# Layer norms of a four-layer decoder trunk: root and reciprocal on whole rows in place of five-column statistics

## Chip, cores and metric

The kernel runs as one launch on one core of a Trainium2 chip (trn2). The metric is the time of one execution on the device in microseconds; smaller is better. Engines are named as the profile names them: PE is TensorE's matmul stream and PEld its weight loads, DVE is VectorE, ACT is ScalarE, POOL is GpSimd, SP is SyncE, which issues the weight loads from memory.

## What is computed

The reference is one inference step of a trunk of four layers over 512 prompt tokens and 8 decode tokens, 520 columns in all, with a model width of 1024. Layers 0 and 3 mix tokens by multi-scale retention, layer 1 by causal pooling over windows, layer 2 by sparse attention that a small indexer selects. After each mixer and after each SwiGLU stands a residual with a layer norm, so there are eight norms. The part that matters here:

```python
def layer_norm(x, g, b):
    xf = x.astype(F32)
    mu = jnp.mean(xf, axis=-1, keepdims=True)
    var = jnp.mean(jnp.square(xf - mu), axis=-1, keepdims=True)
    return ((xf - mu) * lax.rsqrt(var + LN_EPS) * g.astype(F32) + b.astype(F32)).astype(x.dtype)

def deepnorm_residual(x, h, g, b):
    return layer_norm(DEEPNORM_ALPHA * x + h, g, b)
...
        xp = deepnorm_residual(xp, hp, ln_g[i, 0], ln_b[i, 0])
...
        xp = deepnorm_residual(xp, swiglu(xp, ffn_w_in[i], ffn_w_out[i]), ln_g[i, 1], ln_b[i, 1])
```

## The kernel before

The activations lie transposed: `x` holds 128 rows of partitions by 8 chunks of 520 columns, so a token is a column and its 1024 features are spread over 128 partitions and 8 chunks. A sum over features is therefore a matmul with the constant matrix `avg`, which gives every partition the mean over all of them.

All large products are made in a three-term split. A weight block of 128 rows by 1024 columns (a *unit*) is loaded by SP into one of four slots of `w_raw`. ACT rounds it to its high part (`split_hi`, L514 to L518), DVE subtracts to get the low part (`split_lo`, L520 to L526), and PE then makes 48 matmuls of 260 columns from it (`multiply`, L536 to L549). `split_next` (L528) splits the unit that stands two places ahead, as soon as the products of the present one are done. The high and low parts have two halves of a ring as their home, so a unit normally has to wait until the unit two places before it is multiplied; `home` (L508) gives only unit 2 of the stage `first` a third place.

Every engine has its own program, a list of stages, and they meet at semaphores. A norm, `norm0a` to `norm3b` (a after the mixer, b after the SwiGLU), goes as follows before the change:

- The last products of the stage before are added to `x` chunk by chunk on DVE (`z_add`, L1732, L1763, L2235 or L2237). After each, DVE adds the chunk to `sum_s` (L1462) and its square, which ACT makes at L1076, to `sum_q` (L1465).
- PE (`norm`, L2958) fills its waiting time with idle products (`hold`, L2955; not in `norm0b` and `norm3b`), spreads the mean over all partitions with `avg` (L2966) and then makes mean and mean square once more in turned form: for five groups of 128 columns it gives one column each (L2972), so that the 520 numbers stand as 128 rows by 5.
- DVE (`norm`, L2253) subtracts the mean from the first four chunks (`less_mean`, L2259), works out the variance on 128x5 (L2267 to L2274); ACT takes the root (L1383), DVE the reciprocal (L2276).
- PE spreads the 128x5 back to all partitions and 520 columns with 12 small products (L2983).
- DVE multiplies each chunk by that (L2307) and, between two of these, subtracts the mean from one of the remaining three chunks and makes the low part of a normed chunk (`x_lo`, L1436). ACT applies gain and bias and makes the high part (L1389, L881).
- PE starts the next stage with `multiply_first` (L563 to L592), which follows the chunks of `x_h` and `x_l` as they come (L578).

One unit of the next stage's weights is split on DVE behind the reciprocal (L524).

The stage `idx` (layer 2, `index`, L2654 on PE) projects four units for the indexer; the first three are turned by a rotation product (L2652, `d_rotate` on DVE, L1821 to L1824). The stage `ret` (layers 0 and 3) starts on ACT with the scaling of the whole `x` by the residual factor (L896).

## Time and profile before

| quantity | value |
|---|---|
| time, median of 3 runs | 3108.71 us (3106.39 to 3112.1) |
| the profiled execution's own time | 3100.85 us |
| its span, first to last instruction | 3099.2 us |
| PE busy | 2963.1 us, 96% |
| PEld busy | 2789.9 us, 90% |
| DVE busy | 2022.0 us, 65% |
| ACT busy | 1250.1 us, 40% |
| POOL busy | 209.1 us, 7% |
| mean granted TensorE clock | 0.976 |

Busy shares are shares of the span. The granted clock is a share of 2.4 GHz: 1.00 is 2.4 GHz, 0.50 is 1.2 GHz, and a value between them is a mean over a stretch in which both occurred. Matmuls overlap, so where the text needs what one matmul costs, it takes the distance between starts and not the duration.

### The profile page before, as it was taken

What the parts mean: (1) busy time and instruction counts of PE and PEld (TensorE: products, weight loads), DVE (VectorE), ACT (ScalarE), POOL (GpSimd) and SP (SyncE); (2) the same over time, 40 slices, a digit from 0 to 9 for tenths busy, and PEclk for the clock granted to TensorE, in tenths of its full rate; (3) what the DMA queues carried; (4) which work ended last, traced back from release to release, by engine and by line L of the source; (5) the groups of instructions that cost most, each with busy time, mean ns of one, the idle gap of its engine ahead of it and who ended that gap; (6) DMA issues with size and microseconds to landing.
All of it is one profiled execution on the core that took longest, in us unless ns stands there. A gap on an engine that the chain in (4) does not pass through costs nothing.

```text
span 3099.2 us, 54122 instructions
## 1 busy us (share of the span) xinstructions
PE 2963.1 (96%) x22655; PEld 2789.9 (90%) x22655; DVE 2022.0 (65%) x3062; ACT 1250.1 (40%) x1881; POOL 209.1 (7%) x342
## 2 busy tenths in 40 slices
PE   7999999999996999998898899999999999999998
PEld 7898987899995999987797799999989888899998
DVE  4555556858567856767886486857555554685766
ACT  3332342535344634433343153534533333263543
POOL 0102111000000000011011100000020111000000
PEclk9999999999997999999998999999999999999998
DMA  6344444233331333332122423333344534323332
GB/s 155 130 126 154 132 131 131 79 103 103 96 92 39 89 96 109 91 99 58 50 74 79 133 69 103 103 96 96 99 144 125 162 126 149 109 82 97 109 94 64
DMA packets 492948, 323.77 MB, mean 104 GB/s; under 512 B 29723, under 2 KB 469275, under 8 KB 492698
## 3 DMA queue, kind: packets, MB, share of 16 engines
q1 hardware_dynamic: 465906, 230.14, 26.6%
q0 software_dynamic: 26800, 90.18, 8.4%
q8 instruction: 180, 2.95, 0.4%
q14 instruction: 62, 0.51, 0.1%
HBM read 275.90 MB, written 44.82 MB: 103 GB/s over the span
## 4 chain that ended last, share of the span: by engine, by line
PE 89%; DVE 7%; ACT 2%; issue 2%; DMA 0%; POOL 0%; DVEq 0%; SPq 0%; ACTq 0%; POOLq 0%
PE ps L547 46%; PE ps L2887 8%; PE ps L2888 8%; PE ps L2889 8%; PE ps L2345 2%; PE ps L597 2%; PE ps L578 2%; PE ps L598 2%; PE ps L599 2%; PE ps L2478 2%; PE ps L2468 1%; ACT w_h L518 1%; DVE wf L2259 1%; DVE wf L2307 1%; PE ps L2972 1%
## 5 line engine op out<-in xcount | busy, mean ns | idle before, releaser
L547 PE MATMUL ps<-rr,w_h 128*128 128x260 f32 x3776 | 608.7, 283 | 1.0 <-DVE rr L2073 1.0
L524 DVE TENSOR_TENSOR w_l<-w_raw,w_h 128x1024 fp32r<-128x1024 f32 (+2 forms) x312 | 336.7, 1079 | 402.2 <-ACT w_h L518 401.1
L547 PEld LDWEIGHTS ps<-rr,w_h 128*128 128x128 f32 x3776 | 518.0, 189 | 7.7 <-issue 5.6
L518 ACT ACTIVATE w_h<-w_raw 128x1024 fp32r<-128x1024 f32 (+2 forms) x312 | 293.3, 940 | 487.0 <-PE ps L547 458.6
L547 PE MATMUL ps<-x_h,w_h 128*128 128x260 f32 x2128 | 443.9, 290 | 7.6 <-DVE w_l L524 5.2
L547 PE MATMUL ps<-x_h,w_l 128*128 128x260 f32 x2128 | 430.9, 284 | 0.0
L547 PE MATMUL ps<-x_l,w_h 128*128 128x260 f32 x2128 | 430.6, 284 | 0.0
L547 PE MATMUL ps<-rr,w_l 128*128 128x260 f32 x1888 | 380.9, 283 | 0.0
L2887 PE MATMUL ps<-x_h,w_h 128*128 128x260 f32 x1280 | 362.0, 283 | 2.2 <-DVE w_l L2111 2.2
L2888 PE MATMUL ps<-x_l,w_h 128*128 128x260 f32 x1280 | 361.5, 282 | 0.0
L2889 PE MATMUL ps<-x_h,w_l 128*128 128x260 f32 x1280 | 361.0, 282 | 0.0
L547 PEld LDWEIGHTS ps<-x_h,w_h 128*128 128x128 f32 x2128 | 332.0, 191 | 32.3 <-issue 23.7
L547 PEld LDWEIGHTS ps<-x_l,w_h 128*128 128x128 f32 x2128 | 331.3, 190 | 0.0
L547 PEld LDWEIGHTS ps<-x_h,w_l 128*128 128x128 f32 x2128 | 330.6, 190 | 0.0
L547 PEld LDWEIGHTS ps<-rr,w_l 128*128 128x128 f32 x1888 | 291.7, 189 | 0.0
L2887 PE MATMUL ps<-rr,w_h 128*128 128x260 f32 x960 | 271.2, 282 | 1.2 <-ACT wf L1301 0.9
L2888 PE MATMUL ps<-rr,w_h 128*128 128x260 f32 x960 | 270.7, 282 | 0.0
L2889 PE MATMUL ps<-rr,w_l 128*128 128x260 f32 x960 | 270.3, 282 | 0.0
L2887 PEld LDWEIGHTS ps<-x_h,w_h 128*128 128x128 f32 x1280 | 240.8, 188 | 3.1 <-DVE w_l L2111 3.1
L2889 PEld LDWEIGHTS ps<-x_h,w_l 128*128 128x128 f32 x1280 | 241.5, 189 | 0.0
L2888 PEld LDWEIGHTS ps<-x_l,w_h 128*128 128x128 f32 x1280 | 240.8, 188 | 0.0
L1258 ACT ACTIVATE w_h<-w_raw 128x1024 fp32r<-128x1024 f32 x160 | 169.7, 1061 | 134.5 <-PE ps L2889 100.6
(349 smaller groups left out, 5017.0 us busy)
## 6 DMA issues: line engine op xcount, KB each, us to landing
w_raw<-in_ffn_w_in SPq DMA_DIRECT2D x176, 512.0 KB, 4.1
w_raw<-in_ret_w_in SPq DMA_DIRECT2D x96, 512.0 KB, 3.8
out<-wf POOLq DMA_DIRECT2D x72, 512.0 KB, 3.5
wf<-in_state_ret POOLq DMA_DIRECT2D x64, 512.0 KB, 5.7
w_raw<-in_ffn_w_out SPq DMA_DIRECT2D x64, 512.0 KB, 4.3
w_raw<-in_ret_w_out SPq DMA_DIRECT2D x64, 256.0 KB, 2.9
w_raw<-in_dsa_w_in SPq DMA_DIRECT2D x27, 512.0 KB, 3.8
w_raw<-in_ffn_w_out SPq DMA_DIRECT2D x32, 384.0 KB, 3.6
```

The source lines that it names most:

```text
L518: C.activation(whole(stage, k, home(w_h, stage, k, n)[:, 0:m]), landed(stage, k, n, m), ACT.Copy).then_inc(S["w_hi"], 1)
L524: V.tensor_tensor(whole(stage, k, home(w_l, stage, k, n)[:, 0:m]), landed(stage, k, n, m), whole(stage, k, home(w_h, stage, k, n)[:, 0:m]. ...
L547: mm = M.matmul(ps[:, 2 * (n % 2) + b, 0:HALF], lhs[:, c, :], rhs[:, c, cols], start=(c == 0 and term == 0), stop=(c == cs - 1 and term == 2))
L578: mm = M.matmul(ps[:, 2 * n + b, 0:HALF], lhs, rhs[:, c, cols], start=(c == 0 and term == 0), stop=(c == DC - 1 and term == 2))
L597: M.matmul(out, lhs_h, rhs_h, start=start, stop=False)
L598: M.matmul(out, lhs_h, rhs_l, start=False, stop=False)
L599: return M.matmul(out, lhs_l, rhs_h, start=False, stop=stop)
L1258: C.activation(w_h[:, a * Q:e * Q], src[:, 0:(e - a) * Q], ACT.Copy).then_inc(S[f"g{g}_hi"], 1)
L2345: return M.transpose(out, src, ident[0:n, 0:n])
L2887: M.matmul(out, wh, hi[:, c], start=fresh and c == 0, stop=False, skip_group_check=True)
L2888: M.matmul(out, wh, lo[:, c], start=False, stop=False, skip_group_check=True)
L2889: mm = M.matmul(out, wl, hi[:, c], start=False, stop=c == 3, skip_group_check=True)
```

## The change

Six things change together.

1. PE no longer makes the turned statistics and no longer spreads the 128x5 back. It spreads the mean and the mean square over all partitions and 520 columns with `avg`, into four banks.
2. The last chunk is not added to `sum_s` and `sum_q` by DVE. PE adds it, as a second accumulating product of `avg` with `x[:, 7]` and with its square.
3. ACT squares the mean (520 columns), DVE forms the variance, clamps it, ACT takes the root and DVE the reciprocal, all on 128x520.
4. `EARLY` goes from 4 to 2: two chunks have their mean subtracted before the reciprocal, and six between the products behind it. The splits of the next stage's first two units move: one to the head of the norm, one behind the first multiplication by the reciprocal.
5. Unit 2 of `idx` and `ret` gets the third home, as `first` has it, and is split at the head of its stage. The order of rotations, copies and splits in `idx` changes.
6. The scaling of `x` in `ret` moves on ACT from the head of the stage to the place behind the fifth unit's evacuation.

The diff, cut to its core:

```diff
-EARLY = 4
+EARLY = 2
...
+        def third(stage, i, k):
+            return kind_of(stage) in ("first", "idx", "ret") and (i, k) == (0, 2)
...
-            if then and kind_of(then[0]) != "fast":
+            if then and kind_of(then[0]) != "fast" and not third(*then):
...
             def ret(stage):
                 act.wait_ge(*at0("x_hi", 0))
-                C.activation(x[:], x[:], ACT.Copy, scale=ALPHA).then_inc(S["xs"], 1)
+                split_hi(act, stage, 0, 2)
...
                     step(4, lambda: raw_v(0))
+                    if i == 0:
+                        C.activation(x[:], x[:], ACT.Copy, scale=ALPHA).then_inc(S["xs"], 1)
...
             def norm(stage, which):
                 at = marks.here(stage)
-                act.wait_ge(*at("ln_v", 4))
-                C.activation(lve, lve, ACT.Sqrt).then_inc(S["ln_sd"], 1)
+                act.wait_ge(*at("stat", 1))
+                C.activation(halves(mean_q), ps[:, 4:6, 0:HALF], ACT.Square).then_inc(S["ln_m"], 1)
+                act.wait_ge(*at("ln_v", 2))
+                C.activation(sum_q, sum_q, ACT.Sqrt).then_inc(S["ln_sd"], 1)
...
+                if m == DC - 1:
+                    return
                 dve.wait_ge(*at("sum_s", m))
...
             def index(stage):
                 at = marks.here(stage)
                 dve.wait_ge(*at("tab_in", 80))
-                for k in range(4):
-                    split_next(split_lo, dve, stage, 0, k)
-                    if k < 3:
-                        d_rotate(at, k, itab, k % 2, k % 2)
...
+                split_lo(dve, stage, 0, 2)
+                for k in range(3):
+                    d_rotate(at, k, itab, k % 2, k % 2, 4 + 2 * (k % 2))
+                    if k == 0:
+                        split_next(split_lo, dve, stage, 0, 1)
...
+                    if k < 2:
+                        split_next(split_lo, dve, stage, 0, k + 2)
...
             def norm(stage):
...
-                dve.wait_ge(*at("stat", 1))
-                dve.wait_ge(*at("sum_q", 0))
+                last = last_unit(stage)
+                if last:
+                    split_next(split_lo, dve, *last[0:2], last[2] - 1)
+                dve.wait_ge(*at("stat", 2))
+                dve.wait_ge(*at("ln_m", 1))
+                V.scalar_tensor_tensor(halves(sum_q), ps[:, 6:8, 0:HALF], EPS, halves(mean_q), ALU.add, ALU.subtract
+                                       ).then_inc(S["ln_v"], 1)
+                dve.wait_ge(*at("ln_v", 1))
+                V.tensor_scalar(sum_q, sum_q, EPS, None, ALU.max).then_inc(S["ln_v"], 1)
                 for c in range(EARLY):
                     less_mean(c)
-                dve.wait_ge(*at("stat", 2))
-                V.tensor_copy(lve, mean).then_inc(S["ln_v"], 1)
...
                 dve.wait_ge(*at("ln_sd", 1))
-                V.reciprocal(lrs, lve).then_inc(S["ln_rs"], 1)
-                if last_unit(stage):
-                    split_next(split_lo, dve, *last_unit(stage))
+                V.reciprocal(sum_q, sum_q).then_inc(S["ln_rs"], 1)
...
-                less_mean(EARLY)
-                dve.wait_ge(*at("ln_b", 1))
+                dve.wait_ge(*at("ln_rs", 1))
...
-                    V.tensor_tensor(halves(ln_e[:, c]), halves(ln_e[:, c]), ps[:, 6:8, 0:HALF], ALU.mult
+                    V.tensor_tensor(halves(ln_e[:, c]), halves(ln_e[:, c]), halves(sum_q), ALU.mult
                                     ).then_inc(S["ln_e"], 1)
-                    if c + EARLY + 1 < DC:
-                        less_mean(c + EARLY + 1)
+                    if c + EARLY < DC:
+                        less_mean(c + EARLY)
+                    if c == 0 and last:
+                        split_next(split_lo, dve, *last)
...
             def index(stage):
...
+                for k in range(2):
+                    pe.wait_ge(*at("d_raw", k + 1))
+                    rotate(at, k, roti, k % 2, 4 + 2 * k)
+                multiply(pe, stage, 0, 2, x_h, x_l, DC)
+                multiply(pe, stage, 0, 3, x_h, x_l, DC, range(2))
+                pe.wait_ge(*at("d_raw", 3))
+                pe.wait_ge(*at("d_rope", 3))
+                rotate(at, 2, roti, 0)
+                multiply(pe, stage, 0, 3, x_h, x_l, DC, range(2, DC))
...
             def norm(stage, before):
-                pe.wait_ge(*at("sum_s", 0))
-                for b, cols in enumerate(prompt_halves()):
-                    mm = M.matmul(ps[:, 4 + b, 0:HALF], avg[:], sum_s[:, cols], start=True, stop=True)
-                mm.then_inc(S["stat"], 1)
...
-                if held:
-                    hold(10)
...
+                for bank, total, added, part, ready in ((4, sum_s, "sum_s", x[:, DC - 1], "z_add"),
+                                                        (6, sum_q, "sum_q", sq[:, (DC - 1) % 2], "sq")):
+                    pe.wait_ge(*at(added, 0))
+                    for b, cols in enumerate(prompt_halves()):
+                        M.matmul(ps[:, bank + b, 0:HALF], avg[:], total[:, cols], start=True, stop=False)
+                    pe.wait_ge(*at(ready, 0))
+                    for b, cols in enumerate(prompt_halves()):
+                        mm = M.matmul(ps[:, bank + b, 0:HALF], avg[:], part[:, cols], start=False, stop=True)
                     mm.then_inc(S["stat"], 1)
```

What moves in the instruction lists is shown at three places. The first is DVE in `norm1b`, from the statistics to the first low part; `x` is the residual stream, `ps` the matmul banks, `w_l` the weights' low parts, and `wf` and `tiny` are work buffers. Before:

```order
L2259 TENSOR_TENSOR wf<-x,ps 128x520 [waits sum_q,stat]
L2259 TENSOR_TENSOR wf<-x,ps 128x520 x3
L2267 COPY tiny<-ps 128x5 [waits stat]
L2269 TENSOR_TENSOR tiny<-tiny 128x5 [waits ln_v]
L2272 TENSOR_TENSOR tiny<-ps,tiny 128x5 [waits ln_v,stat]
L2274 TENSOR_SCALAR tiny<-tiny 128x5 [waits ln_v]
L2276 RECIPROCAL tiny<-tiny 128x5 [waits ln_sd]
L524 TENSOR_TENSOR w_l<-w_raw,w_h 128x1024 [waits w_hi]
L2259 TENSOR_TENSOR wf<-x,ps 128x520
L2307 TENSOR_TENSOR wf<-wf,ps 128x520 [waits ln_d,ln_b]
L2259 TENSOR_TENSOR wf<-x,ps 128x520
```

And with the change:

```order
L526 TENSOR_TENSOR w_l<-w_raw,w_h 128x1024 [waits w_hi,z_add]
L2280 SCALAR_TENSOR_TENSOR wf<-ps,wf 128x520 [waits ln_m,stat]
L2283 TENSOR_SCALAR wf<-wf 128x520 [waits ln_v]
L2272 TENSOR_TENSOR wf<-x,ps 128x520 x2
L2287 RECIPROCAL wf<-wf 128x520 [waits ln_sd]
L2315 TENSOR_TENSOR wf<-wf 128x520 [waits ln_d,ln_rs]
L2272 TENSOR_TENSOR wf<-x,ps 128x520
L526 TENSOR_TENSOR w_l<-w_raw,w_h 128x1024 [waits w_hi]
L2315 TENSOR_TENSOR wf<-wf 128x520 [waits ln_d]
L2272 TENSOR_TENSOR wf<-x,ps 128x520
L1445 TENSOR_TENSOR x_l<-x,x_h 128x520 [waits x_n,x_hi]
```

Five instructions on 128x5 and the wait for PE's spreading (`ln_b`) have gone; the reciprocal is 520 wide, and one split has moved in front of the statistics and one behind the first multiplication.

The second place is PE in the same norm, from its idle products (L2955, now L2965) on. Before, up to the first of the twelve products that spread the 128x5 (thirteen more idle products follow them):

```order
L2955 MATMUL ps<-ident_r 128x256 x10
L2966 MATMUL ps<-wf,avg 128x260 [waits sum_s]
L2966 MATMUL ps<-wf,avg 128x260
L2972 MATMUL ps<-avg,wf 128x1 [waits sum_s]
L2972 MATMUL ps<-avg,wf 128x1 x4
L2972 MATMUL ps<-avg,wf 128x1 [waits sum_q]
L2972 MATMUL ps<-avg,wf 128x1 x4
L2955 MATMUL ps<-ident_r 128x256 x10
L2983 MATMUL ps<-ident,tiny 128x128 [waits ln_rs]
```

And with the change, up to the thirteen idle products:

```order
L2965 MATMUL ps<-ident_r 128x256 x10
L2978 MATMUL ps<-wf,avg 128x260 [waits sum_s]
L2978 MATMUL ps<-wf,avg 128x260
L2981 MATMUL ps<-x,avg 128x260 [waits z_add]
L2981 MATMUL ps<-x,avg 128x260
L2978 MATMUL ps<-wf,avg 128x260 [waits sum_q]
L2978 MATMUL ps<-wf,avg 128x260
L2981 MATMUL ps<-wf,avg 128x260 [waits sq]
L2981 MATMUL ps<-wf,avg 128x260
L2965 MATMUL ps<-ident_r 128x256 x13
```

Eight wide products stand in place of two wide and sixteen narrow ones, the ten idle products in the middle have gone, and the thirteen at the end now follow the statistics and not the spreading.

The third place is DVE at the head of `idx`, in the change; `wf` holds the rotated projections, and the three splits L526 without a wait for `tab_in` are those of unit 3 and of units 0 and 1 of the following stage `q`. The second rotation is the second row of L1833:

```order
L526 TENSOR_TENSOR w_l<-w_raw,w_h 128x1024 [waits w_hi,tab_in]
L1833 TENSOR_TENSOR wf<-ps,wf 128x520 [waits d_rope,rot]
L1834 TENSOR_TENSOR wf<-wf 128x520
L1836 TENSOR_TENSOR wf<-wf 128x520 [waits d_rope]
L526 TENSOR_TENSOR w_l<-w_raw,w_h 128x1024 [waits w_hi]
L1848 COPY wf<-wf 128x8 [waits d_rope]
L1851 TENSOR_TENSOR rr<-wf,rr 128x520 [waits d_hi]
L526 TENSOR_TENSOR w_l<-w_raw,w_h 128x1024 [waits w_hi]
L1833 TENSOR_TENSOR wf<-ps,wf 128x520 [waits d_rope,rot]
```

Before, the split of `q`'s unit 0 stood behind the second rotation and ahead of the third; now it stands ahead of the second, and that of unit 1 ahead of the third.

## Rows read from the trace of the kernel before

**Rows 1.** The profile page: the chain that ended last, by engine.
```profile
PE 89%; DVE 7%; ACT 2%; issue 2%; DMA 0%; POOL 0%; DVEq 0%; SPq 0%; ACTq 0%; POOLq 0%
```

**Rows 2.** Timeline of norm1b: start us, us, engine, line, operation, [idle before <-releaser].
```profile
1355.83 1.48 PE L2955 MATMUL ps<-ident_r 128*128 128x256 f32 x11
1356.03 0.70 DVE L2235 TENSOR_TENSOR x<-ps,x 128x520 f32<-128x520 f32 x1 [0.74 <-PE ps L547]
...
1357.52 1.14 PE L2966 MATMUL ps<-wf,avg 128*128 128x260 f32 x4 [0.21 <-DVE wf L1462]
1358.50 2.51 PE L2972 MATMUL ps<-avg,wf 128*128 128x1 f32 x20
...
1362.23 0.19 DVE L2276 RECIPROCAL tiny<-tiny 128x5 f32<-128x5 f32 x1 [0.27 <-ACT tiny L1383]
1362.33 1.18 DVE L524 TENSOR_TENSOR w_l<-w_raw,w_h 128x1024 fp32r<-128x1024 f32 x1
...
1364.91 0.69 DVE L2307 TENSOR_TENSOR wf<-wf,ps 128x520 f32<-128x520 f32 x1 [0.79 <-PE ps L2983]
1365.53 0.69 DVE L2259 TENSOR_TENSOR wf<-x,ps 128x520 f32<-128x520 f32 x1
```

**Rows 3.** Groups of instructions by line and form: count | busy us, mean ns of one.
```profile
L1482 DVE TENSOR_TENSOR wf<-wf,rtab 128x1040 f32<-128x1040 f32 x16 | 19.8, 1236 | 0.6
...
L2011 DVE RECIPROCAL tiny<-tiny 128x1 f32<-128x1 f32 x32 | 4.5, 142 | 5.8 <-ACT wf L1222 5.8
L2276 DVE RECIPROCAL tiny<-tiny 128x5 f32<-128x5 f32 x8 | 1.5, 190 | 2.2 <-ACT tiny L1383 1.9 <-ACT tiny L1366 0.3
...
L2274 DVE TENSOR_SCALAR tiny<-tiny 128x5 f32<-128x5 f32 x8 | 1.4, 170 | 0.3
...
L1532 DVE TENSOR_SCALAR wf<-wf,headc 128x520 f32<-128x520 f32 x32 | 15.4, 480 | 0.0
...
L1076 ACT ACTIVATE wf<-x 128x520 f32<-128x520 f32 x64 | 40.1, 627 | 42.0 <-DVE x L2235 17.8 <-DVE x L1763 11.8 <-DVE x L1732 7.4
```

**Rows 4.** Timeline of norm2a, norm0a, norm1a, norm0b: idle products or last addition, first multiplication.
```profile
1793.30 1.47 PE L2955 MATMUL ps<-ident_r 128*128 128x256 f32 x11
...
1801.51 0.69 DVE L2307 TENSOR_TENSOR wf<-wf,ps 128x520 f32<-128x520 f32 x1
...
549.48 1.52 PE L2955 MATMUL ps<-ident_r 128*128 128x256 f32 x11
...
562.14 0.70 DVE L2307 TENSOR_TENSOR wf<-wf,ps 128x520 f32<-128x520 f32 x1 [1.92 <-PE ps L2983]
...
986.71 2.71 PE L2955 MATMUL ps<-ident_r 128*128 128x256 f32 x11 [6.28 <-DVE x L1763]
...
998.14 0.69 DVE L2307 TENSOR_TENSOR wf<-wf,ps 128x520 f32<-128x520 f32 x1 [2.25 <-PE ps L2983]
...
920.04 0.70 DVE L2235 TENSOR_TENSOR x<-ps,x 128x520 f32<-128x520 f32 x1 [1.71 <-PE ps L547]
...
929.67 0.70 DVE L2307 TENSOR_TENSOR wf<-wf,ps 128x520 f32<-128x520 f32 x1 [1.65 <-PE ps L2983]
```

**Rows 5.** Timeline behind norm0a: PE's first product after `multiply_first`.
```profile
578.97 0.40 PE L547 MATMUL ps<-x_h,w_h 128*128 128x260 f32 x2
```

**Rows 6.** Stretches: us, busy per engine (x), PEclk, DMA share, GB/s; behind norm2a and norm2b.
```profile
1811.00:1815.00 4.00, 4.00 (x22) 4.00 (x22) 2.97 (x5) 3.94 (x6) 0.00 (x0) 0.58 0.00 0
2192.00:2195.00 3.00, 3.00 (x21) 3.00 (x21) 2.97 (x3) 0.00 (x0) 0.00 (x0) 0.71 0.96 345
```

**Rows 7.** Timeline: PE at unit 2 of `ret0` and `ret3`, then first rotation and transposes of `idx`.
```profile
39.41 0.48 PE L547 MATMUL ps<-x_h,w_h 128*128 128x260 f32 x2 [0.91 <-DVE w_l L524]
...
2191.74 0.48 PE L547 MATMUL ps<-x_h,w_h 128*128 128x260 f32 x2 [3.20 <-DVE w_l L524]
...
1382.64 1.04 PE L2652 MATMUL ps<-wf 128*128 128x260 f32 x4
...
1403.87 2.24 PE L2345 MATMUL ps<-ident,wf 128*128 128x128 f32 x10 [0.84 <-ACT wf L1118]
```

More of the change, by code:

```diff
@@ L373, in trunk @@
         ve, rs, mhalf = tiny[:, 40:45], tiny[:, 45:50], tiny[:, 50:51]
-        lve, lrs = tiny[:, 51:56], tiny[:, 56:61]
         hist, inv, tail = wf[:, 6240:7264], wf[:, 7264:7328], wf[:, 7328:8352]
@@ L506, in arrived, with home @@
             return S[f"w_in{slot_of(stage, i, k)}"], (marks.unit(stage, i, k) // 4 + 1) * 16
-        def home(w, stage, k, n):
-            if (kind_of(stage), k) == ("first", 2):
+        def third(stage, i, k):
+            return kind_of(stage) in ("first", "idx", "ret") and (i, k) == (0, 2)
+        def home(w, stage, i, k, n):
+            if third(stage, i, k):
                 return w[:, 5 * Q:7 * Q]
@@ L517, in split_hi @@
             act.wait_ge(*arrived(stage, i, k))
-            C.activation(whole(stage, k, home(w_h, stage, k, n)[:, 0:m]), landed(stage, k, n, m), ACT.Copy).then_inc(S["w_hi"], 1)
+            C.activation(whole(stage, k, home(w_h, stage, i, k, n)[:, 0:m]), landed(stage, k, n, m), ACT.Copy).then_inc(S["w_hi"], 1)
         def split_lo(dve, stage, i, k):
@@ L541, in multiply @@
                 pe.wait_ge(*unit_mark("w_lo", stage, i, k))
[L542 to L543 removed]
+            wh = home(w_h, stage, i, k, n).rearrange("p (c n) -> p c n", n=P)
+            wl = home(w_l, stage, i, k, n).rearrange("p (c n) -> p c n", n=P)
             for c in part:
@@ L1121, in index @@
                 at = marks.here(stage)
-                for k in range(4):
-                    if k >= 2:
-                        act.wait_ge(*at("d_rope", 3 * (k - 2) + 3))
-                    d_copy(at, k, stage, 0, k, k % 2)
-                    split_next(split_hi, act, stage, 0, k)
-                    if k < 3:
-                        act.wait_ge(*at("d_rope", 3 * k + 3))
-                        C.activation(qi_h[:, k, :] if k < 2 else ki_h, d_f[:, k % 2], ACT.Copy).then_inc(S["d_hi"], 1)
+                split_hi(act, stage, 0, 2)
+                d_copy(at, 0, stage, 0, 0, 0)
+                d_copy(at, 1, stage, 0, 1, 1)
+                split_next(split_hi, act, stage, 0, 1)
+                for k in range(3):
+                    act.wait_ge(*at("d_rope", 3 * k + 3))
+                    C.activation(qi_h[:, k, :] if k < 2 else ki_h, d_f[:, k % 2], ACT.Copy).then_inc(S["d_hi"], 1)
+                    if k < 2:
+                        d_copy(at, k + 2, stage, 0, k + 2, k)
+                        split_next(split_hi, act, stage, 0, k + 2)
                 act.wait_ge(*at("wi_tp", 1))
@@ L1345, in down @@
                 for k in range(8):
-                    if last and k == 7:
-                        square(at, at, k)
                     if k < 6 or not then:
@@ L1354, in down @@
                         lone_hi(stage, then)
-                    if last and k < 7:
+                    if last:
                         square(at, at, k)
@@ L1381, in norm @@
                 at = marks.here(stage)
-                act.wait_ge(*at("ln_v", 4))
-                C.activation(lve, lve, ACT.Sqrt).then_inc(S["ln_sd"], 1)
+                act.wait_ge(*at("stat", 1))
+                C.activation(halves(mean_q), ps[:, 4:6, 0:HALF], ACT.Square).then_inc(S["ln_m"], 1)
+                act.wait_ge(*at("ln_v", 2))
+                C.activation(sum_q, sum_q, ACT.Sqrt).then_inc(S["ln_sd"], 1)
                 for c in range(DC):
@@ L2254, in norm @@
                 at = marks.here(stage)
-                mean, square = (ps[:, 6 + n, STAT_AT:STAT_AT + QT + 1] for n in range(2))
                 def less_mean(c):
@@ L2659, in index @@
                 pe.wait_ge(*at("tab_in", 80))
-                for k in range(4):
-                    if k >= 2:
-                        pe.wait_ge(*at("d_raw", k - 1))
-                        multiply(pe, stage, 0, k, x_h, x_l, DC)
-                    if k < 3:
-                        pe.wait_ge(*at("d_raw", k + 1))
-                        if k:
-                            pe.wait_ge(*at("d_rope", 3 * k))
-                        rotate(at, k, roti, k % 2)
+                for k in range(2):
[7 more added lines that the diff above has]
+                multiply(pe, stage, 0, 3, x_h, x_l, DC, range(2, DC))
                 pe.wait_ge(*at("d_rope", 9))
```

71 lines of the change are left out of this document (25 added, 46 removed).

## Prediction, before the change was run

> **What bounds the kernel now.** I read the page first. The chain that ended last runs on PE for 89% of the span and on DVE for 7% [rows 1], so the kernel is one long stream of matmuls, and time is gained or lost only where PE has nothing useful to do. Such places are the norms and the heads of `ret` and `idx`, so I went through the timeline there.
>
> One norm shows the order of things [rows 2]. In `norm1b` the last chunk is added at 1356.03 and done 0.70 us later, at 1356.73. PE passes its idle products (from 1355.83, 1.48 us), spreads the mean at 1357.52, makes narrow statistics from 1358.50. The reciprocal on 128x5 starts at 1362.23. After PE has spread it back, DVE multiplies the first chunk at 1364.91, and PE's first useful product follows as soon as ACT has scaled it. The reader should see two distances: from the last addition to the first multiplication (8.2 us here), which the change rebuilds, and from the first multiplication to the end of `multiply_first`, which depends on how quickly DVE delivers chunks. The second is 578.97 - 562.14 = 16.83 us in `norm0a` [rows 4, 5].
>
> **New path up to the first multiplication.** PE: a product of 260 columns with `avg` runs as two passes. Four passes start at 1357.52 and the next row starts at 1358.50 [rows 2], so a pass takes 0.245 us. The change has 8 products, 16 passes, 3.92 us in a row behind the idle products, which take 1.38 us from start to the next free place; with 0.15 us until the result can be read, the mean square stands 5.45 us after the first idle product.
>
> Then comes a chain that is 520 wide throughout. DVE waits for the semaphore (0.05), forms the variance, priced as a 520-wide two-tensor operation (0.69 [rows 2]), waits again (0.04), clamps (0.48 at L1532 [rows 3], of which about 0.42 until the next can start) and subtracts two means (two times 0.61, the distance of 1364.91 and 1365.53 [rows 2]). That makes 2.42 us until the reciprocal can start. The root on ACT, priced as its 520-wide square, 0.63 [rows 3], runs beside the two subtractions and is ready first. ACT's square of the mean and the root's table load lie beside PE's last eight passes (8 x 0.245 = 2.0 us) and cost nothing; without that cover they would add up to those 2 us.
>
> **The reciprocal's price R decides.** No row shows a wide one. For ordinary operations width costs 1.05 ns per element: 0.69 us at 520 [rows 2], 1.236 at 1040 [rows 3]. At that rate and with nothing else, R is 0.69 us: the lower bound. The reciprocal goes from 142 ns at one element to 190 at five [rows 3], 12 ns per element, which gives 142 ns + 519 x 12 ns = 6.4 us: the upper bound. A nearer reading is what it occupies: the split behind the five-wide reciprocal starts 0.10 us later (1362.23, 1362.33 [rows 2]). A 520-wide operation occupies 0.61 us, 0.54 for its elements and about 0.065 fixed. So five elements take 0.035 to 0.04 us, 7 to 8 ns each, and 520 take about 4.2 us; with fixed part and tail **R = 4.4 us**. I take this, because it compares the same operation in the same place with the instruction behind it, and durations of tiny operations contain waits.
>
> A rule speaks to this. The Trainium skill, "VectorE: DVE Perf Modes", section "First, the fixed hardware budget", says that reciprocal is an iterative divide with a repeat count of 8. By it R would be about eight times the 0.54 us of a plain row, 4.3 us as an estimate, and by the plain row's own price 0.69: the sum below would differ by 29 us. The five-wide row sides with the rule, though it is only five wide.
>
> So the first multiplication stands 5.45 + 2.42 + 4.4 = 12.27 us after the first idle product. Norm by norm, against the old start [rows 2, 4]:
>
> - `norm1b`: 1355.83 + 12.27 = 1368.10 against 1364.91, +3.2. `norm2b` is of the same build, +3.2.
> - `norm2a`: 1793.30 + 12.27 = 1805.57 against 1801.51, +4.1.
> - `norm1a`: PE comes from 6.28 us without work and runs the idle products at half rate, 2.71 us instead of 1.48 [rows 4], that is at 1.2 GHz. I let half of the passes run so: 5.5 us instead of 3.92 and 2.75 for the idle products, 986.71 + 15.2 = 1001.9 against 998.14, +3.8.
> - `norm0a`: 549.48 + 12.27 = 561.75 against 562.14, -0.4; here DVE was late with its sums, and not adding the last chunk saves that. `norm3a` alike, -0.4.
> - `norm0b` has no idle products; four passes are done before the last addition ends at 920.74 and 12 follow: 920.74 + 0.05 + 2.95 + 0.15 + 2.42 + 4.4 = 930.7 against 929.67, +1.0. `norm3b` alike, +1.0.
>
> Sum: **+15.5 us**. This part moves by 8 us for each us of R.
>
> **Behind the first multiplication** DVE now subtracts six means instead of three and makes a split. Each chunk costs it three operations of 0.61, 1.83 us, against about 1.45 that ACT and PE need for one (12 products of 0.121). The second multiplication starts at 0.61 + 0.61 + 1.14 (the split) = 2.36, the seventh 5 x 1.83 later at 11.5, the eighth at 12.7. Its high part is ready at about 15.1 and PE then has 32 products left, 3.9 us: 19.1 us against 16.83, +2.25 in `norm0a`, `1b`, `2a`, `2b`, `3a`; without the split 18.0 in `norm1a`, +1.1. In `norm0b` three subtractions and a half-wide split go ahead of the last chunk, +2.1, and in `norm3b`, where PE's transposes hide part, +1.0. Sum: **+15.5 us**. It does not depend on R.
>
> **The heads of the stages.** In `ret3` PE waits 3.20 us for unit 2's low part and then runs at a granted clock of 0.71 (a mean of 1.2 and 2.4 GHz) [rows 6, 7] for two such stretches of 3 us: with the third home the wait goes, and 6 us x 0.29 = 1.7 with it, **-5 us**. In `ret0` the wait is 0.91 [rows 7], **-0.9**. The moved scaling is eight 520-wide rows of ACT, at most 8 x 0.63 = 5 us by [rows 3]. It now stands beside PE's unit 5, 48 products of 0.12, 5.75 us, and so costs nothing; if ACT came to it late, it could delay one evacuation by 1 to 2 us in each of the two stages. In `idx` PE gets from the first rotation at 1382.64 to the transposes at 1403.87 [rows 7], 21.2 us. Now: two rotations 2.0, unit 2 5.75, two chunks of unit 3, a rotation and the rest 6.75, done at 14.5. But DVE now has the split of `q`'s unit 0 ahead of the second rotation, and ACT cannot make its high part before unit 2 is multiplied: unit 2 ends at 7.75, ACT's copy and split take 1.65 (0.63 per 520 [rows 3]) and DVE's split 1.18 [rows 2], so DVE resumes at 10.6. The same follows behind unit 3 (14.5 + 2.85 = 17.4), and the third rotation, three operations of DVE, ends at 19.4. The stall is thus not removed but moved to the transposes: -1.9, of which PE, starting again at 1.2 GHz, takes about 0.9, **-1**.
>
> **Clock.** PE's thirteen idle products end about 7 us before its first product now. A stretch like that is followed by 1.2 GHz in `norm1a`. But in the next 10 us DVE sets the pace, and I charge +2 in all. In return `norm2a` already lost time so (0.58 over 4 us [rows 6]) and `norm1b` a little; that is now hidden behind DVE, -3.
>
> **Sum:** 15.5 + 15.5 - 5 - 0.9 - 1 + 2 - 3 = **+23 us**. On the profiled execution's own 3100.85 us that is 3123.9. This execution lies 7.9 us below the median of 3108.71 and below all three runs (3106.39 to 3112.1), so I put the sum on the median: **3131.7, say 3131 us**.
>
> **Rivals.**
> A. *The reciprocal streams like any wide row*, R = 0.69. Then 8 x 3.71 = 29.7 us go and the time is 3102. For it: 190 ns at five elements is only 20 ns more than the 170 of the scalar operation of the same width [rows 3], which a fixed surcharge would explain. Against it: the start-to-start distance. It decides from R below 0.75 us on; at 1.5 us the change is worth nothing. The Trainium skill, "Vector Engine (DVE) Microarchitecture Reference", section "3.2 Anatomy of a single slice", has the divide chain span all eight slices, which reads as one element per cycle and would give this case; no row here is wide enough to show it.
> B. *Something between*, R near 2 us: +3.8, 3112, no change that can be measured.
> C. *R as forecast or up to 6.4, and PE stays at 1.2 GHz through `multiply_first`.* Then PE needs 2.6 us per chunk, 25.6 us in place of 19.1, six norms by some 3 to 6.5: 3145 to 3170. For it: 7 us without work in six norms. Against it: 11 idle products brought `norm1a` back to 2.4 GHz.
>
> **How the numbers follow.** A measurement of this kernel tells changes of over 0.2%, 6.2 us, from none. Forecast 0.56 (3119 to 3140 by the bounds of the unmeasured parts), A 0.24, B 0.10, C 0.10. A lies at the edge of 0.2%: 0.19 of it faster, 0.05 the same. Faster 0.19, same 0.15 (B and that part of A), slower 0.66. The range of 8 in 10 runs from 3100, inside A, to 3145, where C begins; the forecast's own is 3119 to 3140.
>
> **What would show it.** Right: a reciprocal row of 128x520 at 4 to 5 us, eight times; first multiplications 10 to 12 us after the last addition in `norm1b` and `norm2a`; chunks in `multiply_first` 1.8 us apart with PE waiting on `x_h`; no wait before unit 2 in `ret3`; a wait of some 5 us before the transposes in `idx`. Wrong: a reciprocal row under 1 us, or a time under 3115.

## The result, and the profile of the changed kernel

The change makes the kernel **slower by about 11 us**: median 3118.62 us (3114.83 to 3122.28, 6 runs) beside 3106.67 us (3102.74 to 3112.1) of the kernel before on the same chip, a ratio of 1.0035, interval 1.0024 to 1.0046. The forecast was 3131 us (+23), range 3100 to 3145: direction and range hold, the size is off by half. The profiled execution took 3114.83 us, its span is 3112.3 us, 13.1 us more than before; the granted clock is 0.973 against 0.976. Both profiles are of the fastest execution that their kernel has here.

The page of the changed kernel: its span, the busy time of the engines, and the chain that ended last by engine:

```profile
span 3112.3 us, 53632 instructions
...
PE 2943.1 (95%) x22435; PEld 2764.5 (89%) x22435; DVE 2041.6 (66%) x3030; ACT 1260.5 (41%) x1889; POOL 209.1 (7%) x342
...
PE 87%; DVE 9%; ACT 2%; issue 2%; DMA 0%; POOL 0%; SPq 0%; DVEq 0%; ACTq 0%; POOLq 0%
```

PE works 20 us less than before (its old statistics were two wide and ten narrow products a norm, not sixteen as counted above, and six products spread the 128x5 in twelve passes) and holds a smaller share of the chain; DVE's share went from 7% [rows 1] to 9%. Its groups by form (busy us, mean ns of one) show with what:

```profile
L2287 DVE RECIPROCAL wf<-wf 128x520 f32<-128x520 f32 x8 | 27.2, 3395 | 0.0
L2272 DVE TENSOR_TENSOR wf<-x,ps 128x520 f32<-128x520 f32 x64 | 43.5, 689 | 0.0
```

The price that was in doubt is 3.40 us, eight times. Plain rows of the same width cost 0.69. The timeline of `norm1b` after, which answers to [rows 2]:

```profile
1360.46 1.48 PE L2965 MATMUL ps<-ident_r 128*128 128x256 f32 x11
1360.66 0.70 DVE L2250 TENSOR_TENSOR x<-ps,x 128x520 f32<-128x520 f32 x1 [1.97 <-PE ps L549]
1361.39 1.23 DVE L526 TENSOR_TENSOR w_l<-w_raw,w_h 128x1024 fp32r<-128x1024 f32 x1
...
1361.78 1.04 PE L2978 MATMUL ps<-wf,avg 128*128 128x260 f32 x4
1362.66 1.04 PE L2981 MATMUL ps<-x,avg 128*128 128x260 f32 x4
...
1365.49 0.70 DVE L2280 SCALAR_TENSOR_TENSOR wf<-ps,wf 128x520 f32<-128x520 f32 x1 [2.87 <-PE ps L2981]
...
1367.78 3.39 DVE L2287 RECIPROCAL wf<-wf 128x520 f32<-128x520 f32 x1
1371.21 0.70 DVE L2315 TENSOR_TENSOR wf<-wf 128x520 f32<-128x520 f32 x1
...
1372.43 1.22 DVE L526 TENSOR_TENSOR w_l<-w_raw,w_h 128x1024 fp32r<-128x1024 f32 x1
...
1373.57 0.69 DVE L2315 TENSOR_TENSOR wf<-wf 128x520 f32<-128x520 f32 x1
1373.75 0.77 PE L580 MATMUL ps<-x_h,w_h 128*128 128x260 f32 x2 [6.76 <-DVE w_l L526]
...
1375.40 0.69 DVE L2315 TENSOR_TENSOR wf<-wf 128x520 f32<-128x520 f32 x1
```

The reader should see three things. DVE waits 2.87 us (the bracket at 1365.49) while PE spreads the means, although it still has a split of weights to make, which it makes at 1372.43, on the path. The first multiplication comes 10.75 us after the first idle product (1371.21 - 1360.46). And the chunks behind it are 1.83 us apart (1373.57, 1375.40), three DVE operations each.

**Where the 13.1 us of the span arose.** For each norm I read, in both timelines, the start of the last product ahead of it, of DVE's first multiplication, and of the last product of `multiply_first` (in `norm0b` and `norm3b`, which have none, of the last multiplication). Distances in us, before and after:

| norm | to the first multiplication | change | forecast | from there to the end | change | forecast |
|---|---|---|---|---|---|---|
| 0a | 12.78, 10.89 | -1.89 | -0.4 | 16.71, 19.03 | +2.32 | +2.25 |
| 0b | 9.95, 9.73 | -0.22 | +1.0 | 6.07, 8.52 | +2.45 | +2.1 |
| 1a | 17.99, 18.73 | +0.74 | +3.8 | 16.69, 17.88 | +1.19 | +1.1 |
| 1b | 9.20, 10.87 | +1.67 | +3.2 | 17.61, 19.02 | +1.41 | +2.25 |
| 2a | 8.33, 10.86 | +2.53 | +4.1 | 19.24, 19.03 | -0.21 | +2.25 |
| 2b | 10.16, 10.87 | +0.71 | +3.2 | 16.71, 19.02 | +2.31 | +2.25 |
| 3a | 12.77, 10.94 | -1.83 | -0.4 | 16.72, 19.09 | +2.37 | +2.25 |
| 3b | 9.98, 9.79 | -0.19 | +1.0 | 7.27, 9.11 | +1.84 | +1.0 |
| sum | | **+1.5** | +15.5 | | **+13.7** | +15.5 |

The norms together cost 15.2 us more. The right half agrees with the forecast (its -3 for the clock in `1b` and `2a` shows there too); the left half is wrong by 14 us. The heads gained 0.9 us in `ret0`, 4.9 in `ret3` and 0.4 in `idx` (taken to the end of `proj`), 6.2 in all. The remaining +4 lies where nothing was changed: +3.3 later in `ret3`, +1.6 later in `ret0`, -0.6 in the pooling. Most of the 3.3 is in the last head of `ret3`. Stretches there, after and then before (columns as in [rows 6]):

```profile
2680.00:2686.00 6.00, 6.00 (x36) 5.69 (x35) 3.43 (x6) 2.14 (x4) 0.00 (x0) 0.72 0.15 44
2686.00:2692.00 6.00, 3.90 (x20) 3.81 (x20) 2.80 (x6) 0.86 (x2) 0.00 (x0) 0.72 0.17 44
```

```profile
2670.00:2676.00 6.00, 4.95 (x40) 4.61 (x40) 5.21 (x9) 2.98 (x5) 0.00 (x0) 1.00 0.15 45
2676.00:2682.00 6.00, 3.90 (x32) 3.70 (x32) 3.18 (x7) 1.19 (x3) 0.00 (x0) 1.00 0.16 46
```

The same instructions, with the same short waits of PE for DVE (1.05 and 2.10 us) among them, ran at a granted clock of 1.00 before and 0.72 after (a mean of 2.4 and 1.2 GHz). That took 3.0 us, and 0.3 a little earlier, back out of the 4.9. The tail of `ret0` lost its 1.6 the same way (0.72 from 522 to 528 us, where the kernel before had 1.00).

### The profile page after: what moved, and what is told of

The parts are those of the page before. It is cut to its first block, busy times and chain, and to the rows that moved or that the text cites. A ratio compares the mean times of both kernels' runs of the same rounds, so it can differ in the third digit from the quotient of the medians.

```text
span 3112.3 us, 53632 instructions
## 1 busy us (share of the span) xinstructions
PE 2943.1 (95%) x22435; PEld 2764.5 (89%) x22435; DVE 2041.6 (66%) x3030; ACT 1260.5 (41%) x1889; POOL 209.1 (7%) x342
## 4 chain that ended last, share of the span: by engine, by line
PE 87%; DVE 9%; ACT 2%; issue 2%; DMA 0%; POOL 0%; SPq 0%; DVEq 0%; ACTq 0%; POOLq 0%
PE ps L549 45%; PE ps L2897 8%; PE ps L2898 8%; PE ps L2899 8%; PE ps L2355 2%; PE ps L599 2%; PE ps L600 2%; PE ps L601 2%; PE ps L2488 2%; PE ps L580 2%; DVE wf L2272 1%; DVE wf L2315 1%; DVE wf L2287 1%; PE ps L2478 1%; ACT w_h L520 1%
## 5 line engine op out<-in xcount | busy, mean ns | idle before, releaser
L526 DVE TENSOR_TENSOR w_l<-w_raw,w_h 128x1024 fp32r<-128x1024 f32 (+2 forms) x312 | 337.1, 1081 | 390.1 <-ACT w_h L520 385.1
## 6 DMA issues: line engine op xcount, KB each, us to landing
w_raw<-in_ffn_w_in SPq DMA_DIRECT2D x176, 512.0 KB, 4.0
w_raw<-in_ret_w_in SPq DMA_DIRECT2D x96, 512.0 KB, 3.9
out<-wf POOLq DMA_DIRECT2D x72, 512.0 KB, 3.6
wf<-in_state_ret POOLq DMA_DIRECT2D x64, 512.0 KB, 5.4
w_raw<-in_ffn_w_out SPq DMA_DIRECT2D x64, 512.0 KB, 4.3
w_raw<-in_dsa_w_in SPq DMA_DIRECT2D x27, 512.0 KB, 3.9
```

What stands on the lines that cost most here:

```text
L526: V.tensor_tensor(whole(stage, k, home(w_l, stage, i, k, n)[:, 0:m]), landed(stage, k, n, m), whole(stage, k, home(w_h, stage, i, k, n)[:, ...
```

## Experiments

Twelve runs, eleven new kernels and the changed kernel once more, each beside the kernel before on the same chip. The median of the kernel before was 3106.52 us beside `recip_more`, `act_arsqrt`, `split_early` and `heads_only`, and 3107.03 beside the others. Distances per norm below run from the last product ahead of the norm to the last of `multiply_first`, as in the table (both halves added).

**More reciprocal** (`recip_more`). The first 260 columns are inverted twice more.

```diff
                 V.reciprocal(sum_q, sum_q).then_inc(S["ln_rs"], 1)
+                for n in (1, 2):
+                    dve.wait_ge(*at("ln_rs", n))
+                    V.reciprocal(sum_q[:, 0:HALF], sum_q[:, 0:HALF]).then_inc(S["ln_rs"], 1)
...
-                dve.wait_ge(*at("ln_rs", 1))
+                dve.wait_ge(*at("ln_rs", 3))
```

> The changed kernel with the reciprocal of the first 260 columns taken twice more behind the one of 520 (the value stays the same). Theory (DVE's chain sets the norms, and a reciprocal costs 6.5 ns per element): two rows of 128x260 of 1.7 to 1.75 us each, first multiplications 3.5 us later in all eight norms, chunks behind them still 1.83 us apart, so 8 x 3.5 = 28 us more: 3118.6 + 28 = 3146.6 us (3143 to 3150). Rival 1 (TensorE's clock sets them: the longer pause costs a longer stretch at 1.2 GHz): over 3155. Rival 2 (part of the reciprocal is hidden beside other work): under 3135.

Measured: 3141.51 us (3141.23 to 3141.84), ratio 1.0111, interval 1.0096 to 1.0126. Its groups by form:

```profile
L2290 DVE RECIPROCAL wf<-wf 128x260 f32<-128x260 f32 x16 | 28.4, 1778 | 0.5
L2287 DVE RECIPROCAL wf<-wf 128x520 f32<-128x520 f32 x8 | 27.1, 3394 | 0.0
```

Two widths give the line: (3394 - 1778) / 260 = 6.2 ns per element and 162 ns fixed. The norms grew by 3.6 us each (`norm1b` 33.52 against 29.89; `norm1a` 4.7), 30 us by the timelines in all eight. The total rose by 23 only: `ret3` took 3.3 us less here, its last head running at full rate, and this kernel's median lies 0.3 us above its profiled execution, that of the changed kernel 3.8. Rival 1 is out. The total is under the range of the theory and over that of rival 2; the norms themselves, where the two differ, show no part of the reciprocal hidden.

**Root and reciprocal in one ACT operation** (`act_arsqrt`). In exact arithmetic the result is the same.

```diff
-                C.activation(sum_q, sum_q, ACT.Sqrt).then_inc(S["ln_sd"], 1)
+                C.activation(sum_q, sum_q, ACT.Abs_reciprocal_sqrt).then_inc(S["ln_sd"], 1)
...
-                dve.wait_ge(*at("ln_sd", 1))
-                V.reciprocal(sum_q, sum_q).then_inc(S["ln_rs"], 1)
...
-                dve.wait_ge(*at("ln_rs", 1))
+                dve.wait_ge(*at("ln_sd", 1))
```

> The changed kernel with root and reciprocal in one ACT operation (absolute value, reciprocal, root), without DVE's reciprocal. Theory (the reciprocal lies wholly on the path): the first multiplications come 3.4 to 3.8 us sooner in all eight norms, 8 x 3.7 = 30 us: 3118.6 - 30 = 3089 us (3086 to 3093), which would be 17 us below the kernel before. Rival (the time behind the pause is TensorE's clock, or PE's first product waits for the split of weights instead): 3100 to 3112.

Measured: 3090.49 us (3089.62 to 3093.5), ratio 0.995, interval 0.9937 to 0.9962. Its timeline in `norm1b`:

```profile
1357.92 0.64 ACT L1392 ACTIVATE wf<-wf 128x520 f32<-128x520 f32 x1 [1.05 <-DVE wf L2283]
1359.02 0.69 DVE L2313 TENSOR_TENSOR wf<-wf 128x520 f32<-128x520 f32 x1
...
1361.55 0.77 PE L580 MATMUL ps<-x_h,w_h 128*128 128x260 f32 x2 [3.33 <-DVE w_l L526]
```

The operation takes 0.64 us on ACT, as the plain root did, and the pause of PE falls from 6.76 to 3.33 us. Seven norms are shorter by 3.2 to 3.5 us and `norm1a` by 2.4, and the total lies inside the theory's range: in seven norms the reciprocal lay wholly on the path.

**The second split moved ahead**, to right behind the first (`split_early`).

```diff
                     split_next(split_lo, dve, *last[0:2], last[2] - 1)
+                    split_next(split_lo, dve, *last)
...
-                    if c == 0 and last:
-                        split_next(split_lo, dve, *last)
```

> The changed kernel with DVE's second split of weights moved from behind the first multiplication to right behind the first split, into the 1.9 to 2.9 us in which DVE waits for the mean square. Theory (behind the first multiplication DVE's work sets the end of multiply_first): the split disappears from the chain, 1.15 us less in norm0a, 1b, 2a, 2b and 3a and half of it in norm0b, 6.4 us in all: 3118.6 - 6.4 = 3112 us (3110 to 3114), and first multiplications at the same distance from the idle products, 10.75 us. Rival (PE at 1.2 GHz needs the time anyway, or the split delays the variance): 3117 to 3121.

Measured: 3107.26 us (3105.25 to 3111.41), ratio 1.0006, interval 0.9997 to 1.0014. In `norm1b`:

```profile
1359.16 2.36 DVE L526 TENSOR_TENSOR w_l<-w_raw,w_h 128x1024 fp32r<-128x1024 f32 x2
...
1363.25 0.70 DVE L2281 SCALAR_TENSOR_TENSOR wf<-ps,wf 128x520 f32<-128x520 f32 x1 [1.73 <-PE ps L2980]
```

Both splits stand ahead of the variance, DVE still waits 1.73 us there, and the first multiplication keeps its distance (1368.97 - 1358.22 = 10.75 us). Each of the five norms with a whole split is 1.14 to 1.25 us shorter, `norm0b` 0.6. The total fell by 11 to 13 us (from 3118.6 and 3120.0), more than the 6.4 expected and to below the theory's range. The norms' own timelines gained 5.5. The profile further has 4 us less in stages that the edit doesn't touch (`ret0` 0.7, the pooling 0.6, `idx` to `proj` 1.4, `ret3` 1.4); `norm1a` took 0.9 more, which the 5.5 contain.

**The changed kernel again** (`after_again`).

> The changed kernel itself once more, beside the others. The four kernels of the first group put its norms and its other stages together to 3112 to 3114 us (3141.5 less eight times 3.6; 3107.3 plus 5.5), 5 us under its own median of 3118.6. Theory (the place in time at which TensorE's clock falls in the stages that nobody changed differs from program to program and stays with the program): 3116 to 3121 us again, with a last head of ret3 in which PE runs at half rate for some 10 us once more. Rival (it was chance of that chip or session): 3111 to 3115.

Measured: 3119.99 us (3115.08 to 3122.95), ratio 1.0044, interval 1.0031 to 1.0057. So the loss came back: `ret3`, from the end of `norm2b` to its last product, takes 513.4 and 513.5 us in the two profiles of the changed kernel. It goes with the program and not with the chip, since on the chip of this second run the next kernel, `hold_long`, takes 510.4 there.

**PE kept busy in the pause** (`hold_long`), with 64 idle products instead of 13.

```diff
-                    hold(13)
+                    hold(64)
```

> The changed kernel with 64 idle products instead of 13 behind the means, so that PE is busy until its first product of the next stage. Theory (behind the first multiplication DVE's 1.83 us per chunk sets the end, PE at 1.2 GHz keeps up or catches up): first products at full rate, ends of multiply_first unmoved, within 0.2 us in each of six norms, total 0 to -3 us. Rival (the pause of 6.7 us is paid for by half the clock behind it, 1 to 3 us in each of six norms): 6 to 18 us less.

Measured: 3119.55 us (3115.02 to 3121.86), ratio 1.0038, interval 1.0026 to 1.005: 0.9 above the changed kernel's first median and 0.4 below its second, so nothing certain gained. Stretches of 4 us behind the pause in `norm1b`, in the changed kernel and then with 64 idle products:

```profile
1373.00:1377.00 4.00, 2.36 (x9) 2.10 (x10) 4.00 (x7) 2.78 (x5) 0.00 (x0) 0.50 0.52 128
1377.00:1381.00 4.00, 3.68 (x16) 3.08 (x15) 4.00 (x8) 3.27 (x5) 0.00 (x0) 0.50 0.02 7
1381.00:1385.00 4.00, 3.95 (x32) 3.74 (x31) 3.66 (x7) 3.27 (x6) 0.00 (x0) 0.95 0.00 0
```

```profile
1376.00:1380.00 4.00, 1.69 (x10) 1.31 (x10) 4.00 (x8) 2.78 (x5) 0.00 (x0) 1.00 0.53 131
1380.00:1384.00 4.00, 3.00 (x15) 2.75 (x16) 4.00 (x7) 3.08 (x5) 0.00 (x0) 0.63 0.00 0
1384.00:1388.00 4.00, 4.00 (x21) 4.00 (x21) 3.66 (x7) 3.45 (x5) 0.00 (x0) 0.52 0.00 0
```

In the changed kernel PE runs at 0.50 in the first two stretches while DVE is busy all of the 4 us and sets the pace, so the half rate costs nothing there. With the idle products the first chunks run at 1.00, PE waits for DVE between them, and the clock falls behind that (0.63, 0.52), where PE has a backlog to work off: `norm1b`, `2a` and `2b` become 1.3 to 1.4 us longer, against the 0.2 that the theory allowed. In this profile `norm1a` was 3 and `idx` to `proj` 2.5 us longer and `ret3` 3 us shorter, so the total alone says little. But the rival is out: removing the pause in front of the products removed no time behind it.

**DVE's order in the norms** (`dve_order`). Both splits first; chunks 0 and 2 have their mean subtracted ahead of the variance, chunk 1 between clamp and reciprocal, while ACT takes the root, and five chunks behind.

```diff
-EARLY = 2
+EARLY = 3
...
+                    split_next(split_lo, dve, *last)
+                dve.wait_ge(*at("stat", 1))
+                dve.wait_ge(*at("ln_m", 1))
+                less_mean(0)
+                less_mean(2)
                 dve.wait_ge(*at("stat", 2))
...
-                for c in range(EARLY):
-                    less_mean(c)
+                less_mean(1)
...
-                    if c == 0 and last:
-                        split_next(split_lo, dve, *last)
```

> The changed kernel with DVE's work moved ahead: the second split right behind the first (as in the run before), two subtractions of the mean ahead of the variance, one between clamp and root, five behind. Theory (from the variance to the last chunk DVE's operations add up): 6.4 us for the splits, and in each of eight norms 0.6 us for one subtraction less behind and 0.3 to 0.5 us in front, 8 us: 3118.6 - 14.5 = 3104 us (3101 to 3107), about the kernel before. Rival (ACT's two operations per chunk, 1.46 us, or PE at half rate take over): 3107 to 3111.

Measured: 3105.48 us (3103.67 to 3107.03), ratio 0.9995, interval 0.9987 to 1.0004. That is within the range, but the norms' own timelines gained 10.6 us (from 223.4 in all eight to 212.8) and not 14.5: 5.5 by the splits, 5 by the subtractions, of which 8 were expected. The rest of the 13 to 14.5 by the medians is not in the norms, so the total met the range in part by luck. `norm2a` and `norm2b` take 28.1 us against 29.89. With a reciprocal of 3.40 us in them the eight norms stay 4.6 us dearer than the old ones (208.2); only `norm0a` and `norm3a` lie below theirs, by 1.2.

**The heads alone** (`heads_only`), on the kernel before (parts 5 and 6 of the change), **and the norms alone** (`norms_only`, parts 1 to 4).

> The kernel before with the third home for unit 2 of idx and ret, the order in idx and the moved scaling alone; norms as before. Theory: the gains of the heads stand by themselves: 4.9 us in ret3, 0.9 in ret0, 0.4 in idx, 3106.7 - 6.2 = 3100.5 us (3098 to 3103). Rival (what a head gains is lost again at the end of ret, where TensorE's clock fell in the profile of the changed kernel): 3105 to 3109.

> The changed kernel's norms with the heads of idx and ret as before (no third home there, the scaling at the head of ret, the old order in idx). Theory (the parts add up: norms +15 us by the profiles, heads -6): 3107 + 15 + 1 = 3123 us (3120 to 3127), with the wait of about 3 us for unit 2's low part back in ret3. Rival (the heads' gain is taken back by TensorE's clock at the end of ret, where the changed kernel runs at half rate): 3117 to 3120, as the changed kernel itself.

Measured: heads alone 3103.55 us (3096.11 to 3110.46), ratio 0.999, interval 0.9979 to 1.0001; norms alone 3119.38 us (3116.99 to 3122.23), ratio 1.0039, interval 1.0025 to 1.0053. The heads' places are as read: in the norms-only kernel the wait ahead of unit 2 in `ret3` stands again, with half rate behind it:

```profile
2205.48 0.77 PE L546 MATMUL ps<-x_h,w_h 128*128 128x260 f32 x2 [2.62 <-DVE w_l L523]
```

But the totals do not add up as expected. Alone the heads bring 3 us instead of 6 (no certain gain), and beside the new norms nothing: 3119.4 without them, 3118.6 and 3120.0 with them. In the heads-only profile `ret3` did gain its 5 us (510.0 us against 515.0), while `idx` to `proj`, of which the edit touches only the head, was 5.4 us longer (416.1 against 410.7), and the norms, which it doesn't touch, 1.7 (209.9 against 208.2: `norm3a` 2.6 longer, `norm2b` 1.9 shorter). The heads alone lie between theory and rival, the norms alone where the rival put them.

**Another order in idx**, in the changed kernel (`idx_order`) and on the heads-only kernel (`heads_idx`).

On ACT (`turned_hi` waits for a turned unit and makes its high part) and then on DVE:

```diff
-                for k in range(3):
...
+                turned_hi(0)
+                turned_hi(1)
+                d_copy(at, 2, stage, 0, 2, 0)
+                split_next(split_hi, act, stage, 0, 2)
+                d_copy(at, 3, stage, 0, 3, 1)
+                turned_hi(2)
+                split_next(split_hi, act, stage, 0, 3)
```

```diff
-                    if k == 0:
-                        split_next(split_lo, dve, stage, 0, 1)
+                    if k != 1:
+                        split_next(split_lo, dve, stage, 0, k or 1)
...
-                    if k < 2:
-                        split_next(split_lo, dve, stage, 0, k + 2)
+                split_next(split_lo, dve, stage, 0, 3)
```

> The changed kernel with another order in idx: ACT makes the high parts of the first two turned units before it copies unit 2, DVE splits q's unit 0 behind the third rotation and q's unit 1 last. Theory (the 4.85 us wait before the transposes comes of DVE standing in the two splits, whose high parts ACT can make only after units 2 and 3 are multiplied): the wait falls to under 1 us, 4 us less there and 1 us more by PE's clock: 3118.6 - 5 = 3113.6 us (3111 to 3116). Rival (the third rotation comes late whatever stands before it, or the stall moves to the first products of q): 3117 to 3120.

> The kernel before with the new heads and the order in idx of the run idx_order; norms as before. Theory (idx_order's gain does not hang on the norms): 3103.6 for the heads alone, less 6 for the wait before the transposes: 3097.5 us (3094 to 3101), the wait under 1 us. Rival (TensorE's clock in the sparse attention takes it back): 3102 to 3105.

Measured: 3110.68 us (3108.37 to 3112.41), ratio 1.0014, interval 1.0005 to 1.0023, and 3093.61 us (3089.11 to 3098.87), ratio 0.9953, interval 0.994 to 0.9967. The transposes in the changed kernel, then with the new order:

```profile
1409.56 3.37 PE L2355 MATMUL ps<-ident,wf 128*128 128x128 f32 x10 [4.85 <-DVE wf L1836]
```

```profile
1407.01 2.23 PE L2360 MATMUL ps<-ident,wf 128*128 128x128 f32 x10 [0.79 <-ACT wf L1123]
```

The wait fell from 4.85 to 0.79 us and the ten transposes, now at full rate, from 3.37 to 2.23: 5.2 us, as expected. The totals fell by 8 to 10 us (to 3110.7 from 3118.6 and 3120.0, and to 3093.6 from 3103.6), each to just below its theory's range; the profiles show 6 to 7 of it between `idx` and `proj`, the rest is not located.

**Both orders** (`dve_idx`)**, and all together** (`best`). The first keeps the reciprocal of 520 columns; the second has the ACT operation in its place.

> The changed kernel with both orders that gained, DVE's in the norms and the one in idx; the reciprocal stays at 520 columns. Theory (independent places): 3105.5 - 8.5 = 3097 us (3094 to 3100). Rival (clock): 3101 to 3106.

> The changed kernel with root and reciprocal in one ACT operation, DVE's work moved ahead as in dve_order, and the order in idx. Theory (the gains add up while DVE sets the pace): 3090.5 less 12 for DVE's order less 8.5 for idx = 3070 us (3066 to 3076), 36 us below the kernel before. Rival (behind a shorter pause PE at half rate, or ACT's 1.46 us per chunk, becomes the bound): 3078 to 3088.

Measured: 3100.73 us (3097.52 to 3103.75), ratio 0.9982, interval 0.9973 to 0.9991, just outside the theory's range and just under the rival's; and 3070.61 us (3069.13 to 3072.2), **ratio 0.9881**, interval 0.9865 to 0.9896, in the middle of it. The last is 36 us below the kernel before and 48 below the changed one. Its `norm1b`:

```profile
1354.39 0.64 ACT L1398 ACTIVATE wf<-wf 128x520 f32<-128x520 f32 x1 [1.21 <-DVE wf L2292]
1355.06 0.70 DVE L2321 TENSOR_TENSOR wf<-wf 128x520 f32<-128x520 f32 x1
...
1356.77 0.48 PE L580 MATMUL ps<-x_h,w_h 128*128 128x260 f32 x2 [2.23 <-ACT x_h L1404]
```

The first multiplication stands 7.06 us behind the first idle product (1348.00) instead of 10.75, and PE pauses for 2.23 us instead of 6.76.

## Why the prediction was right in direction and wrong in size

**What bounds the kernel** held: PE's stream of products, with time lost in the norms, where DVE's chain sets two distances, and in the heads.

**The failed step is the first term, "new path up to the first multiplication": +15.5 us forecast, +1.5 measured.** Four sizes in it were off, by some 8, 3, 2 and 1 us in all.

- *The reciprocal, R = 4.4 us.* Measured 3.40 (first multiplication 3.43 after its start). That is 1.0 us in each of eight norms, **8 of the 14 us**. I had read 7 to 8 ns per element out of a distance of 0.10 us between two starts [rows 2], after taking off 0.065 us as the fixed part of another operation, and had used the 8. At the measured 6.2 ns the five elements are 0.031 us of that distance, so its fixed part is 0.07 us or a little more. Because five elements stand for 520, an error of 0.01 us in the fixed part is 1 us in R. Rounding of the 0.10 is not the cause: in `norm1a` the distance is 0.11 (995.13 and 995.24), by which R would have come out higher still. The slope of the two narrow rows [rows 3], 12 ns, was no better. The bounds of 0.69 and 6.4 were fair; the point in between was not worth its two digits.
- *PE's spreading.* Four passes take 0.88 us (1361.78 to 1362.66), 0.22 each, where I had charged 0.245; the variance starts 5.03 us behind the first idle product, not 5.5. With 0.1 us in the chain behind it, this is 0.5 to 0.6 us in each of five norms (`0a`, `1b`, `2a`, `2b`, `3a`) and 0.2 in `0b` and `3b`, some 3 us in all. R and this turn 12.27 into 10.75 us.
- *`norm1a`.* I let half of the passes run at half rate, 5.5 us for sixteen. In the changed kernel they took 3.5 (991.93 to 995.41 below), and the first multiplication came 12.2 us after the first idle product, 2 us sooner than charged beyond R:

```profile
989.42 2.71 PE L2965 MATMUL ps<-ident_r 128*128 128x256 f32 x11 [6.28 <-DVE x L1775]
...
991.93 1.21 PE L2978 MATMUL ps<-wf,avg 128*128 128x260 f32 x4
...
995.41 1.89 PE L2965 MATMUL ps<-ident_r 128*128 128x256 f32 x13
```

- *`norm2b` before.* I called it "of the same build" as `norm1b` and took its time from there. But in `norm2b` PE spread the 128x5 at a granted clock of 0.50, in 2.56 us against 1.73, and the first multiplication came 10.05 us after the first idle product, against 9.08 in `norm1b`. The row of `norm1b`, then those of `norm2b`:

```profile
1363.15 1.73 PE L2983 MATMUL ps<-ident,tiny 128*128 128x128 f32 x12
...
2168.95 2.56 PE L2983 MATMUL ps<-ident,tiny 128*128 128x128 f32 x12
...
2171.55 0.69 DVE L2307 TENSOR_TENSOR wf<-wf,ps 128x520 f32<-128x520 f32 x1 [1.75 <-PE ps L2983]
```

**On the rule for R.** The wide row now decides between the two readings: a reciprocal does not stream, so rival A is out. The Trainium skill, "VectorE: DVE Perf Modes", section "First, the fixed hardware budget", with its repeat count of 8, pointed the right way; the rows here give 6.2 ns per element against 1.05 of a plain wide row [rows 2, 3], a factor of 6 and not 8.

**Behind the first multiplication** the forecast of +15.5, less 3 for clock that is hidden now, met 13.7. The rows show chunks 1.83 us apart; `split_early` and `dve_order` confirm that the split lay on the path, and `hold_long` that the half rate costs nothing, with a reservation: it is free only as long as DVE is the one that is late.

**The heads** gained what was forecast in their places (6.2 against 6.9; in `idx` the stall did move to the transposes, 4.85 us). That this would arrive at the end was wrong: PE's half rate in untouched code took back 4.9 us in the profile (3.3 in `ret3`, 1.6 in `ret0`) and, by the medians of the kernels with and without the heads, all of it. The sum had no term for that; its +2 for the clock stands for the ten microseconds behind the pause in the norms. It was luck for the total: the first term was 14 us too high, and the +4 of untouched code hid part of that.

**Rivals.** B, R near 2 us and no change, is out by the row itself, although the total came out between B and the forecast. C, PE held at 1.2 GHz to the end of `multiply_first`, is out: the stretches show 0.95 from some 7 us behind the first product on. What I held against C was misread, though. The eleven idle products of `norm1a` had not brought PE back to 2.4 GHz in the kernel before: the four passes behind them still took 2.10 us at half rate, against 1.14 in `norm1b` [rows 2], and the granted clock was back at 1.00 only from about 992 on:

```profile
989.46 2.10 PE L2966 MATMUL ps<-wf,avg 128*128 128x260 f32 x4
```

```profile
992.00:994.00 2.00, 2.00 (x19) 2.00 (x19) 2.00 (x4) 0.00 (x0) 0.00 (x0) 1.00 0.00 0
```

## What to carry to other kernels

An operation whose price per element is not known from a wide row must be priced as a range: the five-wide row gave 4.4 us where 3.40 was measured. If the range decides, choose the change so that it does not matter. Before an operation is widened to save a spreading product, look for another engine that does it at the price of a plain row; here ACT took 0.64 us for what cost DVE 3.40, and with DVE's new order beside it the eight norms, 15 us dearer than before in the changed kernel, came out 20 us cheaper (187.7 us in all against 208.2). Where an engine waits ahead of a long chain and has independent work behind it, move that work into the wait; two such moves took 10.6 us out of the eight norms.
